# A two-block transformer layer on one core: attention scores as fp32r products of high and low parts, two pairs of value products in one place, one scaling moved a step

## What is computed

```python
q = rms_norm(q.reshape(B_, S_, N_HEADS, HEAD_DIM), q_norm_g)
k_s = rms_norm(k_s.reshape(kv_shape), k_norm_g[1])
k_w = rms_norm(k_w.reshape(kv_shape), k_norm_g[2])
kc = rms_norm(compress(k_c.reshape(kv_shape), cmp_pos_k, w_cmp_k), k_norm_g[0])
...
s_c = (jnp.einsum('bsgrd,bcgd->bgrsc', q, kc).astype(jnp.float32) * SCALE
       - slopes[:, :, None, None] * dist_c)
p_c = masked_softmax(s_c, dist_c >= 0)
o_cmp = jnp.einsum('bgrsc,bcgd->bsgrd', p_c.astype(vc.dtype), vc)
...
o_nsa = (g[:, :, 0] * o_cmp + g[:, :, 1] * o_slc + g[:, :, 2] * o_win).reshape(B_, S_, QW)
```

## Time and profile before

| what | value |
|---|---|
| median of 3 runs | 902.2 us |
| the profiled execution's own time | 901.26 us |
| its span | 899.2 us |
| PE busy | 892.7 us (99%) |
| DVE, ACT, POOL busy | 706.0, 555.3, 43.2 us |
| share of PE in the chain that ended last | 99% |
| PE, DVE, ACT busy between 36 and 64 us (28 us) | 28.00, 23.38, 18.73 us |
| PE, DVE, ACT busy between 125 and 180 us (55 us) | 55.00, 48.10, 42.62 us |

### The profile page before, as it was taken

The page is one execution under the profiler, slowest core; times in us unless marked ns, Lnnn a source line. Parts: engine busy times, 40 slices in busy tenths (PEclk is TensorE's granted clock), DMA queues, the critical chain, the costliest instruction groups (busy, mean ns, idle before and its releaser), DMA issues.

```text
span 899.2 us, 13582 instructions
## 1 busy us (share of the span) xinstructions
PE 892.7 (99%) x4926; PEld 767.0 (85%) x4926; DVE 706.0 (79%) x1381; ACT 555.3 (62%) x954; POOL 43.2 (5%) x54
## 2 busy tenths in 40 slices
PE   9999999999999999999999999999999999999997
PEld 7988877888888888888889998888889988888886
DVE  6888899789866666677998999999976786666665
ACT  7767878755644444456655657776745755754454
POOL 0410000000000000000010100100000000000000
PEclk9999999999999999999999999999999999999999
DMA  9977677676465555556798888487565377555551
GB/s 343 320 214 199 177 203 219 198 293 202 154 229 187 192 191 196 190 191 209 219 236 268 231 206 270 106 230 240 169 211 164 114 212 237 187 187 187 188 188 47
DMA packets 97218, 184.53 MB, mean 205 GB/s; under 512 B 8128, under 2 KB 18176, under 8 KB 96896
## 3 DMA queue, kind: packets, MB, share of 16 engines
q1 hardware_dynamic: 92128, 166.35, 56.1%
q0 software_dynamic: 4656, 16.78, 10.0%
q10 hardware_dynamic: 368, 0.52, 0.2%
HBM read 164.69 MB, written 1.05 MB: 184 GB/s over the span
## 4 chain that ended last, share of the span: by engine, by line
PE 99%; ACT 1%; issue 0%; DVE 0%; DVEq 0%; ACTq 0%
PE pb L523 97%; PE pb L527 1%; PE pb L738 1%; ACT SM L1400 0%; ACT wlo L1174 0%; ACT SM L1174 0%; ACT whi L1174 0%; ACT PTC L1174 0%; DVE XS L2617 0%; DVE XS L2625 0%; DVEq L59 0%; DVE DG L2359 0%; ACT MSQ L1757 0%; DVE ST L2603 0%; ACT CC L1174 0%
## 5 line engine op out<-in xcount | busy, mean ns | idle before, releaser
L1174 ACT ACTIVATE whi<-raw 128x1024 fp32r<-128x1024 f32 (+2 forms) x304 | 309.1, 1039 | 125.5 <-PE pb L523 112.5
L1787 DVE TENSOR_TENSOR wlo<-raw,whi 128x1024 fp32r<-128x1024 f32 (+1 forms) x267 | 315.7, 1211 | 78.7 <-ACT whi L1174 78.2
L523 PE MATMUL pb<-XT,whi 128*128 128x512 f32 (+1 forms) x1232 | 283.8, 358 | 0.0
L523 PE MATMUL pb<-whi,ZO 128*128 128x512 f32 (+1 forms) x776 | 238.9, 388 | 0.0
L523 PEld LDWEIGHTS pb<-XT,whi 128*128 128x128 f32 x1232 | 200.8, 189 | 23.8 <-issue 1.4
L523 PEld LDWEIGHTS pb<-whi,ZO 128*128 128x128 f32 x776 | 145.2, 188 | 29.7 <-issue 0.4
L523 PE MATMUL pb<-XT,wlo 128*128 128x256 f32 (+1 forms) x1032 | 166.4, 282 | 0.0
L523 PEld LDWEIGHTS pb<-XT,wlo 128*128 128x128 f32 (+1 forms) x1032 | 153.2, 190 | 14.0
L523 PE MATMUL pb<-whi,XT 128*128 128x512 f32 (+1 forms) x544 | 161.8, 389 | 0.0
L523 PE MATMUL pb<-wlo,ZO 128*128 128x512 f32 (+1 forms) x388 | 148.3, 387 | 0.0
L523 PEld LDWEIGHTS pb<-whi,XT 128*128 128x128 f32 x544 | 101.0, 188 | 20.7 <-issue 0.7
(11 more groups left out here) (258 smaller groups left out, 657.9 us busy)
## 6 DMA issues: line engine op xcount, KB each, us to landing
raw<-in_w_in SPq DMA_DIRECT2D x105, 512.0 KB, 4.8
raw<-in_w_ff SPq DMA_DIRECT2D x64, 512.0 KB, 5.3
raw<-in_w_up SPq DMA_DIRECT2D x32, 512.0 KB, 4.5
raw<-in_w_down SPq DMA_DIRECT2D x32, 512.0 KB, 4.8
wlo<-raw POOLq DMA_DIRECT2D x31, 512.0 KB, 5.8
raw<-in_w_branch_b SPq DMA_DIRECT2D x8, 512.0 KB, 5.3
raw<-in_w_out SPq DMA_DIRECT2D x8, 512.0 KB, 4.1
raw<-in_wx_kv SPq DMA_DIRECT2D x8, 512.0 KB, 5.4
```

The source lines that it names most:

```text
L523: return e.matmul(o, l, r, start=start, stop=stop, skip_group_check=True)
L1174: return e.activation(o, i, ACT.Copy, scale=scale)
L1787: e.tensor_tensor(wlo[u % NW][:, 0:c], raw_tile(u)[:, 0:c], whi[u % NW][:, 0:c].bitcast(F32), ALU.subtract).then_inc(lo, 1)
```

## The change

**Scores.** Queries and keys are split like the weights. `OT`, which stands empty until the first attention sums, holds them: for each head 128 rows, the high part of its query in 64 rows and the low part in the other 64; for each group and kind of key, the high part in both row halves and the low part in both row halves (`q_cols`, `k_cols`). One product over all 128 rows with the keys' high part, and a second with their low part, give all four partial products. ACT makes the high parts from PSUM in four copies of 64 rows per turned bank instead of two of 128; DVE makes the low parts in a new function `qk_low` (four instructions each at s = 3, 4 and 5); POOL issues two DMAs of 64x1024 that double the keys, instead of two of 64x512 that swapped them. The compressed keys get a high and a low part too (`KCS`, in `ZT`), their scores are sixteen products of 32 columns instead of eight of 64, and DVE adds the two parts onto the distances in eight small instructions instead of two (the distances are now loaded right into `PC`).

**Values.** Both pairs of an f are multiplied at one step: 22, 29, 35 and 42. The turned probabilities get a third buffer.

**Scaling.** ACT scales the first head of pair 0 at s = 13 instead of 14.

```diff
-        PTP = [work(W0 + a, f"PT{i}", 768) for i, a in enumerate((12016, 14840))]
+        PTP = [work(W0 + a, f"PT{i}", 768) for i, a in enumerate((12016, 14840, 7216))]
...
-        values_of = {a: (i,) for i, a in enumerate(pair_at[3:] + (35,))}
-        values_of[42] = (6, 7)
-        last_value = {a: n[-1] // 2 for a, n in values_of.items() if n[-1] % 2}
+        values_of = {22: (0, 1), 29: (2, 3), 35: (4, 5), 42: (6, 7)}
+        last_value = {a: n[0] // 2 for a, n in values_of.items()}
...
 # PE, attention1
                         if n >= 2:
-                            e.wait_ge(qk_out, n - 1)
+                            e.wait_ge(*((kc_copied, 1) if n == 2 else (qk_lo, 1)))
...
-                                a = 256 * t + 64 * f
-                                i = mm(PB[7][:, a:a + 64], TT[:, TQ + f, t * P:t * P + P], KCT[:, :],
-                                       t == 0 and f == 0, t == 1 and f == 3)
+                                for p in range(2):
+                                    a, g = 256 * t + 64 * f + 32 * p, f // 2
+                                    i = mm(PB[7][:, a:a + 32].rearrange("p (l n) -> p l n", l=2),
+                                           OT[:, q_cols(f, p)][:, t * P:t * P + P], kcs[:, :, 15 * g:15 * g + 16],
+                                           a == 0, a == 480)
...
                         for p in range(2):
-                            r = slice(64 * p, 64 * p + 64)
-                            mm(PB[4 + p][:, 0:128], TT[r, TQ + f, 0:128], TT[r, k[p], 0:128], True, False)
-                        for p in range(2):
-                            r = slice(64 * p, 64 * p + 64)
-                            mm(PB[4 + p][:, 128:384], TT[r, TQ + f, 128:256], TT[r, k[p], 0:256], False,
+                            q = OT[:, q_cols(f, p)]
+                            mm(PB[4 + p][:, 0:128], q[:, 0:128], OT[:, k_cols(g, 0, b)][:, 0:128], True, False)
+                            mm(PB[4 + p][:, 0:128], q[:, 0:128], OT[:, k_cols(g, 1, b)][:, 0:128], False, False)
+                            mm(PB[4 + p][:, 128:384], q[:, 128:256], OT[:, k_cols(g, 0, b)], False, False)
+                            mm(PB[4 + p][:, 128:384], q[:, 128:256], OT[:, k_cols(g, 1, b)], False,
                                True).then_inc(sc_done, 1)
...
 # ACT, attention1
-                            copy(TT[:, i0, :], PB[4 + n % 2][:, 0:256], g[0])
-                            copy(TT[:, i0 + 1, :], PB[4 + n % 2][:, 256:512], g[1]).then_inc(qk_out, 1)
+                        for j in range(2):
+                            for p in range(2):
+                                r = slice(64 * p, 64 * p + 64)
+                                o = OT[r, q_cols(2 * n - 2 + j, p) if n < 3 else k_cols(p, 0, j)]
+                                i = copy(o, PB[4 + n % 2][r, 256 * j:256 * j + 256], qk_gain(n, j, r))
+                        i.then_inc(qk_hi, 1)
...
-                    if s - 4 in pair_of:
+                    if s == 13:
+                        scale_p(0, 0)
+                    if s - 4 in pair_of and s > 14:
                         scale_p(2 * pair_of[s - 4], 0)
...
 # DVE
+            def qk_low(n):
+                e.wait_ge(qk_hi, n)
+                for j in range(2):
+                    for p in range(2):
+                        r, q = slice(64 * p, 64 * p + 64), slice(64 - 64 * p, 128 - 64 * p)
+                        c = q_cols(2 * n - 2 + j, p) if n < 3 else k_cols(p, 0, j)
+                        o = OT[q, c] if n < 3 else OT[r, k_cols(p, 1, j)]
+                        i = e.scalar_tensor_tensor(out=o, in0=PB[4 + n % 2][r, 256 * j:256 * j + 256],
+                                                   scalar=qk_gain(n, j, r), in1=OT[r, c].bitcast(F32),
+                                                   op0=ALU.mult, op1=ALU.subtract)
+                i.then_inc(qk_lo, 1)
...
+                    if s in (3, 4, 5):
+                        qk_low(s - 2)
...
-                        e.tensor_scalar(KCT[:, :], KCT[:, :], prm("kg"), None, ALU.mult).then_inc(kct_out, 1)
+                        step(e.tensor_scalar(KCS[:, 0:32], KCT[:, :], prm("kg"), None, ALU.mult))
+                        after_step()
+                        e.scalar_tensor_tensor(out=KCS[:, 32:64], in0=KCT[:, :], scalar=prm("kg"),
+                                               in1=KCS[:, 0:32].bitcast(F32), op0=ALU.mult,
+                                               op1=ALU.subtract).then_inc(kct_out, 1)
...
+                        for l in range(2):
+                            if l:
+                                after_step()
+                            for g in range(2):
+                                for q in range(2):
+                                    d = pc[:, :, q, 2 * g:2 * g + 2, 15 * g:15 * g + 15]
+                                    step(e.tensor_tensor(d, cs[:, :, 2 * g:2 * g + 2, q, l, 0:15], d, ALU.add))
...
 # POOL
+            e.wait_ge(qk_lo, 3)
+            for g in range(2):
+                r, q = slice(64 * g, 64 * g + 64), slice(64 - 64 * g, 128 - 64 * g)
+                k = OT[:, 2048 + 1024 * g:3072 + 1024 * g].bitcast(F32)
+                e.dma_start(k[q, :], k[r, :]).then_inc(ks_doubled, 16)
```

More of the change, by code:

```diff
@@ L91, in build @@
         KCN = work(1088, "KCN", 128)
-        KCT = work(1216, "KCT", 64)
+        KCT = work(1216, "KCT", 32)
         KCV = work(1280, "KCV", 256)[:, :].rearrange("p (f n) -> p f n", f=4)
@@ L100, in build @@
         SQ = work(W0 + 2608, "SQ", 1536)
-        TT = work(W0 + 2608, "TT", 3072)[:, :].rearrange("p (i n) -> p i n", i=12)
+        TT = work(W0 + 2608, "TT", 1024)[:, :].rearrange("p (i n) -> p i n", i=4)
         WC = work(W0 + 6704, "WC", 2048)[:, :].rearrange("p (w j e) -> p w j e", w=2, j=16)
@@ L106, in build, with pt1 @@
         SMP = [work(W0 + 10480 + 768 * i, f"SM{i}", 768) for i in range(2)]
-        PTP = [work(W0 + a, f"PT{i}", 768) for i, a in enumerate((12016, 14840))]
+        PTP = [work(W0 + a, f"PT{i}", 768) for i, a in enumerate((12016, 14840, 7216))]
         SM, PT = ([v[i // 2][:, 384 * (i % 2):384 * (i % 2) + 384] for i in range(4)] for v in (SMP, PTP))
-        SM2, PT2 = ([v[i][:, :].rearrange("p (c n) -> p c n", c=6) for i in range(2)] for v in (SMP, PTP))
+        SM2, PT3 = ([v[:, :].rearrange("p (c n) -> p c n", c=6) for v in b] for b in (SMP, PTP))
+        def pt1(j):
+            return PTP[j // 2 % 3][:, 384 * (j % 2):384 * (j % 2) + 384]
         CC = [work(W0 + a, f"CC{i}", 1024)[:, :].rearrange("p (f n) -> p f n", f=4) for i, a in enumerate((12784, 16240))]
@@ L151, in build, with q_cols, k_cols @@
         GF = work(W0, "GF", 1024)
+        KCS = ZT[:, 0:64]
+        def q_cols(f, p):
+            return slice(512 * f + 256 * p, 512 * f + 256 * p + 256)
+        def k_cols(g, l, b):
+            a = 2048 + 1024 * g + 512 * l + 256 * b
+            return slice(a, a + 256)
         ident = CST[:, 0:128]
@@ L407, in build, with qk_gain, key_tile @@
             "cross_scores", "cross_max", "cross_exp", "cross_p", "cross_p_turned", "cross_p_copied", "cross_summed"))
-        TQ, TK, TC = 0, 4, 8
-        def key_tile(first_tile, w, g, half):
-            return first_tile + w + 2 * (g != half)
+        def qk_gain(n, j, r):
+            a = PRM["kg"] + 1 + j
+            return PR[r, a:a + 1] if n == 3 else QG[r, 2 * n - 2 + j:2 * n - 1 + j]
+        def key_tile(w, g, half):
+            return w + 2 * (g != half)
         pair_at = (10, 13, 16, 19, 22, 26, 29, 32)
@@ L879, in attention1 @@
                         n = pair_of[s]
-                        f, k = n // 2, [key_tile(TK, n % 2, n // 4, p) for p in range(2)]
-                        e.wait_ge(qk_out, 4)
-                        e.wait_ge(ks_swapped, 32)
+                        f, b, g = n // 2, n % 2, n // 4
+                        e.wait_ge(qk_lo, 3)
+                        e.wait_ge(ks_doubled, 32)
                         if n:
@@ L1412, in copy_p @@
                 e.wait_ge(pt_done, len(by_pe) + j + 1 if base else by_pe.index(j) + 1)
-                if base + j >= 4:
+                if base:
                     e.wait_ge(pv_done, base + j - 3)
-                copy(PT[j % 4][:, :], PB[5 if base else 6][:, 0:384]).then_inc(pt_out, 1)
+                elif j >= 6:
+                    e.wait_ge(pv_done, j - 5)
+                copy(PT[j % 4] if base else pt1(j), PB[5 if base else 6][:, 0:384]).then_inc(pt_out, 1)
             def make_o_hi(p, bank, done, c=0):
@@ L2006, in attention1 @@
                                 r = slice(64 * half, 64 * half + 64)
-                                v = TT[r, key_tile(TC, w, g, half), 16 * half:16 * half + 240].rearrange(
+                                v = TT[r, key_tile(w, g, half), 16 * half:16 * half + 240].rearrange(
                                     "p (c j) -> p c j", j=16)
@@ L2036, in attention1 @@
                         e.wait_ge(cs_done, 1)
[L2037 to L2044 removed]
```

(6 more changed lines are left out.)

53 lines of the change are left out of this document (22 added, 31 removed).

## The result

The changed kernel took 905.58 us (median of 5 runs, 904.75 to 906.40), the kernel before 902.16 beside it (901.48 to 902.30). The ratio is 1.0042, its interval 1.0031 to 1.0053: slower, and outside the predicted range. The profiled execution took 906.4 us, its span 904.4, and is the slowest of the five; that of before took 901.26, its span 899.2, less than any of the five beside it.

The account below looks back on a forecast made before the run. PE's own instructions were taken to bound the kernel. Gains of 1.1 and 0.4 us against waits of 1.2 and 0.6 gave +0.3 on 902.2, so 902.5 us, range 900.7 to 904.3.

Parts of the forecast that it names:

- Bound and place: PE, busy 892.7 of 899.2 us, bounds the kernel; new waits come ahead of the first products of x0 and x1.
- PE's gain: Attention insertions on PE fall from 16.8 to 15.7 us, score blocks at 0.92 each: 1.1 us gained.
- the rival of the float32 price: Short fp32r products on PE run in two passes, a score block taking 1.36: 907.1 us; chance 0.12.
- the rival of cheaper short products: 128-column products on PE cost 0.085 instead of 0.11: 0.8 us less, 901.7, or 899.9 without waits; chance 0.08.
- The scaling: ACT's earlier scaling of the first head removes PE's wait at pair 0's turn: 0.4 us gained.
- new waits behind 100 us: Sign that would show the forecast wrong: PE waiting anew behind 100 us.
- the first place: Ahead of x0's first product: added ACT and DVE work makes DVE 2.1 us late; PE waits 1.2 us.
- as columns set the time, four take 1.44: ACT's four 64-row copies take 1.44 us where two copies took 0.72, so the next high part starts 0.72 later.
- The cover of 0.9: DVE frees c0's first tile at 46.2, PE starts x0 at 47.14: 0.9 us of lateness costs nothing.
- The turning of the keys just passes: PE's turn of the keys at 46.78 needs the first four low parts, expected by 46.3: no wait.
- Second place: At x1: DVE 2.7 us late, first add_right of c1 ends at 76.2; PE waits 0.6 us (0.2 to 1.3).
- Sum: Whole kernel: -1.1 - 0.4 + 1.2 + 0.6 = +0.3 us, giving 902.5 us, no measurable difference.

Follow-up runs that it names:

- e3: Kernel before with only the values of both pairs in one insertion, third buffer and first head's scaling at s = 13; 901.48 us, 0.9997.
- e13: Kernel before with merged values, scaling at s = 13, and first head of pair 2 scaled at s = 19 instead of 20; 901.18 us, 0.9992.
- e2: Changed kernel with ACT's four copies and DVE's four low parts per bank ordered one row half after the other; 905.39 us, 1.0037.
- e5: Changed kernel with DVE's low parts of queries and keys left out but for one column each; 904.52 us, 1.0026.
- e6: Kernel before with twelve more DVE instructions of the low parts' form and size at s = 3, 4 and 5; 904.01 us, 1.0024.
- e7: Changed kernel with low parts of two more weight units (20 and 21) made by ACT copy and summing DMA instead of DVE; 905.12 us, 1.0035.
- e4: Changed kernel with 24 unused extra products on PE around the keys' turn, filling PE's wait; 905.41 us, 1.0039.
- e9: Changed kernel with both high and low parts of queries and keys left out but for one column each; 902.19 us, 1.0004.
- e14: Kernel before with ACT's copies of queries and keys in four pieces of 64 rows a bank instead of two of 128; 902.40 us, 1.0009.
- e15: Kernel before with ACT's copies in four 64-row pieces and twelve low-part-like instructions on DVE; 906.90 us, 1.0057.
- e10: Changed kernel with ACT's high parts left out but for one column, DVE's low parts full; 905.31 us, 1.0038.
- e1: Changed kernel with DVE's low parts later, keys turned in bank 6, and POOL's doubling DMAs behind its factor; 905.67 us, 1.0046.
- e8: Changed kernel with low and high parts later, keys turned in bank 6, units 20 and 21 by DMA, compressed softmax later on DVE; 909.25 us, 1.0082.

## Why the prediction was wrong, point by point

**Bound and place: right.** PE's own time and its waits decided, and the largest new wait came where it was worked out, ahead of x0, at c0's `add_right`.

**PE's gain: right, a little large.** Compared start by start, PE's regular products are 5.45 us later than before at c1 and 4.66 behind step 35, 0.79 less; 0.37 of that is the scaling's wait, and 0.44 of new wait is in it: PE saves 0.9 us instead of 1.1. A product of 128 columns is one record; the rival of the float32 price is out. That a block measured 0.93 against 0.92 is luck in part: from start to start in the block at 76.13 its four products of 128 columns take 0.35 together and its four of 256 columns 0.58, where 0.44 and 0.48 had been put. So the rival of cheaper short products had their price right (0.09 each), but a block is no shorter for it. The rule of the Trainium skill quoted there ("TensorE: Matmul & The Clock Gate", section "Back-to-back issue gap") would have made a block an estimated 0.80; it measured 0.93. (Two slips in the prediction's sums change nothing: 32 x 0.05 is 1.6 and not 1.5, and 902.2 + 1.3 - 1.8 is 901.7 and not 901.6.)

**The scaling: right.** The wait of 0.37 is gone. But merging the values uncovered another, 0.4 at s = 19, which no step had, one of the new waits behind 100 us that the prediction gave as a sign of being wrong. In e3 the two parts are alone, and the wait is there; in e13 it is gone.

**The failed step is the size of the first place**: "as columns set the time, four take 1.44", and 1.58 for the low parts. Columns do not set the time where consecutive instructions alternate between row halves: four copies take 1.93 (44.33 - 42.40), 0.49 more, four low parts 2.01 (48.68 - 46.67), 0.43 more, and the `wlo` ahead of them 1.25 instead of 1.14. DVE so came to x0's bank 0.49 + 0.43 + 0.11 = 1.03 later than worked out, and where 1.2 us of wait had been put the profile has 1.3 + 1.6. The same thing stood in the earlier trace rows: the `KP` additions, 64 rows in alternating halves, are 0.41 apart for 240 columns, the 128-row `CC<-pb,CC` 0.34 for 256 (these also read PSUM). I used that row to say that 64 rows are not shorter, and not that they are longer. Here a page would have helped: the Trainium skill, "VectorE: DVE Perf Modes", section "Two Vector instructions with no wait between them", has a Vector instruction start only after the earlier ones are finished if an input or the output begins in another group of 32 rows than the one last read or written in that memory. e2 agrees for DVE (0.40 within a half, 0.48 across).

**The cover of 0.9 was too large, and one execution's.** PE does not start when the `add_right` ends but 0.26 later (51.03 - 50.35 - 0.42), so of the 0.9 some 0.67 could be used. And in the changed kernel's profile PE's c0 began 0.55 later than before, but ACT came to the copies 1.39 later (42.40; 41.01 in the earlier trace rows); 0.84 of cover was gone. ACT had waited 2.83 us for a weight unit to land, 1.46 for the same one before, and then 1.04 for another, where before the load had landed in time:

```profile
34.41 1.06 ACT L1192 ACTIVATE whi<-raw 128x1024 fp32r<-128x1024 f32 x1 [2.83 <-DMA raw<-in_w_in]
...
39.83 2.18 ACT L1192 ACTIVATE whi<-raw 128x1024 fp32r<-128x1024 f32 x2 [1.04 <-DMA raw<-in_w_in]
```

With 1.03, 0.26 and 0.84 the predicted 1.2 becomes 3.3. In the trace x0 starts 3.34 later against c0 than before; 1.3 + 1.6 = 2.9 of that are the waits. Such a beginning is not the change's doing: in e3, with no load added ahead of x0, ACT waited 2.67 for the same unit and x0 starts 0.26 after the first `CC<-pb,CC` ends (47.21 + 0.43), with all of the cover spent:

```profile
47.21 1.42 DVE L2136 TENSOR_TENSOR CC<-pb,CC 128x256 f32<-128x256 f32 x4
```

```profile
47.90 0.70 PE L526 MATMUL pb<-XT,whi 128*128 128x512 f32 x2
```

Some loaded kernels spread widely (e5 over 3.9 us, e6 over 3.8; the changed kernel over 1.7, the kernel before over 0.8 to 1.6). That the beginning makes this spread is argued, not shown; in e7 the longer times are those with the lower granted clock.

**"The turning of the keys just passes": wrong**, by 1.3 us, but at no price of its own: without this wait PE would have waited the longer for x0's bank, which DVE frees at the same time either way.

**Second place: mis-sized by the same term, and hidden in one profile.** 0.6 was predicted at x1; where the clock stayed up it was 0.9 (e2) and 1.2 (e4, where x1 starts 1.4 later). The other terms of this place came out; the two further calls of `qk_low` took 2.01 + 2.00 = 4.0 us instead of 3.2:

```profile
52.93 1.98 DVE L2024 SCALAR_TENSOR_TENSOR ZO<-pb,ST,ZO 64x256 fp32r<-64x256 f32 x4
54.94 1.67 DVE L2048 TENSOR_TENSOR KP<-TT,PR 64x240 f32<-64x240 f32 x4
...
58.12 1.98 DVE L2024 SCALAR_TENSOR_TENSOR ZO<-pb,PR,ZO 64x256 fp32r<-64x256 f32 x4
60.12 0.43 DVE L2151 TENSOR_TENSOR CC<-CC,RX 128x256 f32<-128x256 f32 x1
```

Where the clock fell, PE lost 1.5 in x0 instead and did not wait at x1. That a wait can cost clock was no term of the sum.

**Sum.** With the beginning of the earlier trace rows, the predicted +0.3 becomes +0.3 + 1.3 at x0 (1.03 and 0.26) + 0.8 at x1 + 0.2 that PE gains less + 0.4 at s = 19 = +3.0; the medians differ by 3.4. A late beginning and the slow clock come on top in the executions that have them. The two profiled ones differ by 5.2: 0.55 at c0, 3.34 at x0, 1.57 behind it at the low clock, 0.79 less from c1 to step 35, 0.50 more around the wait for a DMA at 180 us (which e9 has too, and e2, e4 and e5 have not). The mechanism held; the waits were sized 1.8 and came to 2.9 at x0 and 1.2 at x1 (e4), 4.1 in all, and the range reached to 2.6, as it took the durations on ACT and DVE as known.

**Open.** How the loss divides between ACT and DVE is no fixed share: put into the kernel before, the two together cost more than the sum of each alone (e14, e6, e15), and with either taken out of the change most of the loss stays (e5, e10). Why some executions begin late is not known. No version with the new scores reached the kernel before. Putting the whole compressed branch behind x1 (its values are wanted only at s = 22) might make the room; this was not tried.

## What to carry to other kernels

A gain of 1 us on the bounding engine was paid for with 19 more instructions on DVE (12 of them low parts) and 6 more on ACT, the first of them ahead of an instruction with 0.9 us of cover: add up the two helpers' loads in one chain, since the second one finds the cover spent. Cost an instruction by a row of the same rows and halves in the same succession, not by its columns. Take from the cover what lies between the end of the instruction that frees and the start of the one that waited, and look at more than one execution for it. A fix that only moves such work (e1, e8) moves the wait with it; what could have paid is work taken out of the stretch.
